# A hybrid decoder layer on one core: turning the next block's rows on VectorE, and branch hints between the job sizes

## What is computed

```
h    = rms_norm(x) * norm_mix
P    = h @ W_in + b_in            -> B_gate | C_gate | u | q | k | v
conv = B_gate * conv3_causal(C_gate * u)
attn = sliding-window attention(QKNorm(q), QKNorm(k), v), 128-query blocks
x    = x + concat(rms_norm(conv), rms_norm(attn)) @ W_out + b_out
x    = x + MoE(rms_norm(x))       top-4 of 32 experts, clamped SwiGLU
```

## Time and profile before

| what | value |
|---|---|
| median of 3 runs | 2038.56 us |
| the profiled execution | 2037.2 us, span 2035.4 us, mean granted TensorE clock 0.990 |
| mixer stage | 0 to about 473 us of the span |
| jobs of over 128 rows | about 501 to 1308 us |
| narrow jobs | about 1308 us to the end |
| TensorE busy | 1977.3 us, 97% of the span |
| VectorE, ScalarE, GpSimd busy | 68%, 19%, 12% |

### The profile page before, as it was taken

How to read it: one execution, slowest core, us unless ns; L and a number is a source line. 1 busy time by engine, 2 the same in 40 slices (tenths; PEclk the granted TensorE clock), 3 DMA queues, 4 the chain that set the end, 5 groups by cost and what they waited for, 6 DMA issues and landing times.

```text
span 2035.4 us, 29772 instructions
## 1 busy us (share of the span) xinstructions
PE 1977.3 (97%) x10588; PEld 1442.1 (71%) x10588; DVE 1385.7 (68%) x3952; ACT 385.3 (19%) x792; POOL 237.5 (12%) x313
## 2 busy tenths in 40 slices
PE   8999999997999999999999999999999999999996
PEld 5777777774999999999999999844444444444443
DVE  2666666663467777778877677687767776677765
ACT  1323233222012122222222222301101010001100
POOL 0221222221010011111111111100000000000000
PEclk9999999998999999999999999999999999999998
DMA  9311110004875687777888888999999999999992
GB/s 302 108 42 41 41 40 12 30 32 182 297 222 198 237 269 243 271 240 274 275 270 286 297 298 289 339 319 366 372 355 363 367 371 362 354 370 369 369 357 76
DMA packets 232241, 504.22 MB, mean 248 GB/s; under 512 B 7428, under 2 KB 14640, under 8 KB 230016
## 3 DMA queue, kind: packets, MB, share of 16 engines
q1 hardware_dynamic: 218496, 454.93, 62.6%
q0 software_dynamic: 11392, 40.18, 8.1%
q10 hardware_dynamic: 2304, 8.39, 1.0%
HBM read 475.48 MB, written 28.00 MB: 247 GB/s over the span
## 4 chain that ended last, share of the span: by engine, by line
issue 44%; PE 26%; DMA 2%; DVE 2%; POOL 1%; ACT 0%; POOLq 0%; DVEq 0%; ACTq 0%
PE ps_unit L1651 26%; DMA out_dram<-y_rows,idx_cur 2%; POOL x_got L1258 1%; DMA x_got<-h_rows,idx_next 0%; DVE act_T L1480 0%; DVE sig L1478 0%; DVE glu L1470 0%; ACT sig L1341 0%; PE ps_list L1623 0%; POOL carrier L1254 0%; POOL out_dram L1302 0%; POOL out_dram L1270 0%; POOLq L1194 0%; DVE match L1391 0%; DVE reached L1435 0%
## 5 line engine op out<-in xcount | busy, mean ns | idle before, releaser
L1651 PE MATMUL ps_unit<-xT,w_slot 128*128 128x136 f32 (+6 forms) x3840 | 526.6, 300 | 10.3 <-issue 8.7
L1651 PEld LDWEIGHTS ps_unit<-xT,w_slot 128*128 128x128 f32 x3840 | 521.3, 197 | 11.5 <-issue 11.4
L1675 PE MATMUL ps_unit<-w_slot,xT 128*128 128x512 f32 x1088 | 473.9, 593 | 0.0
L1675 PEld LDWEIGHTS ps_unit<-w_slot,xT 128*128 128x128 f32 x1088 | 205.3, 190 | 251.6 <-issue 251.6
L1183 DVE STREAM_TRANSPOSE xT<-x_got 32x256 f32<-32x256 f32 x668 | 291.0, 436 | 13.4 <-DMA x_got<-h_rows,idx_next 4.6
L1651 PE MATMUL ps_unit<-act_T,w_slot 128*128 128x136 f32 (+6 forms) x1920 | 264.1, 299 | 7.2 <-DVE act_T L1480 7.1
L1651 PEld LDWEIGHTS ps_unit<-act_T,w_slot 128*128 128x128 f32 x1920 | 259.4, 191 | 10.4 <-DVE act_T L1480 6.3
L1687 PE MATMUL ps_unit<-w_slot,act_T 128*128 128x512 f32 x544 | 239.3, 592 | 1.3 <-DVE act_T L1183 1.3
L1496 DVE STREAM_TRANSPOSE y_rows<-yT 32x256 f32<-32x256 f32 x396 | 172.6, 436 | 42.9 <-ACT yT L1348 37.6
L1183 DVE STREAM_TRANSPOSE act_T<-act_rows 32x64 f32<-32x64 f32 x816 | 192.6, 236 | 12.2
L1687 PEld LDWEIGHTS ps_unit<-w_slot,act_T 128*128 128x128 f32 x544 | 102.0, 190 | 123.6 <-issue 121.5
(11 more groups left out here) (262 smaller groups left out, 1604.3 us busy)
## 6 DMA issues: line engine op xcount, KB each, us to landing
w_slot<-in_w_dram SPq DMA_DIRECT2D x192, 2048.0 KB, 11.0
b_row<-in_b_dram SPq DMA_DIRECT2D x17, 1024.0 KB, 13.0
b_row<-in_b_dram SPq DMA_DIRECT2D x17, 512.0 KB, 15.3
w_in_sb<-in_w_in_dram SPq DMA_DIRECT2D x6, 1024.0 KB, 11.9
x_in<-in_x_dram SPq DMA_DIRECT2D x8, 512.0 KB, 3.4
x_res<-in_x_dram SPq DMA_DIRECT2D x8, 512.0 KB, 4.8
out_dram<-x ACTq DMA_DIRECT2D x8, 512.0 KB, 5.1
h_rows<-h ACTq DMA_DIRECT2D x8, 512.0 KB, 3.1
```

The lines of the kernel that those rows point to most:

```text
L1651: last = pe.matmul(ps_unit[p % RING][:, u, 0:n], w, moving[:, k, 0:n], start=(k == 0), stop=(k == KD - 1))
L1675: last = pe.matmul(ps_hid[c], xT[:, k, 0:P], w_slot[:, c, k, :], start=(k == 0), stop=(k == KD - 1))
```

## The change

Three edits, in both stages.

1. **Rows of the next block.** Squaring (`square_x`) moves to the start of ScalarE's pass and norming (`norm_x`) behind the second u bias; the mean moves behind `add_taps(0)` on VectorE, the reciprocal root to the start of GpSimd's pass. VectorE turns `xn` straight into `hT` in 16 pieces, in three groups of 4, 6 and 6, and ScalarE scales `hT` in place by `norm_mix_col` with 8 instructions. TensorE's two `turn_x` and VectorE's two `read_hT` per pass go, but for block 0. The load of block 1's `x_in` moves up in SyncE's queue, ahead of the store of `rel_rows`, and the two loads in SyncE's loop change places.
[...]
3. **Counts.** Four small matmuls with powers of 64 pack the 12 counts into three numbers; TensorE reads these three words once, between its `hold_clock` matmuls, and unpacks them into registers, in place of one `value_load` before each width.

```
@@ sync
+            wait(sp, x_normed, 0)
+            sp.dma_start(x_in[:], x_rows[P:2 * P, :]).then_inc(x_loaded.sem, 16)
             sp.wait_ge(rel_made, 1)
             sp.dma_start(rel_rows, rel_row).then_inc(rel_stored, 16)
...
-            with sp.Fori(0, NB - 1) as t:
+            with sp.Fori(1, NB - 1) as t:
+                load_residual(t - 1)
                 load_block(t, x_rows[bass.ds((t + 1) * P, P), :])
-                load_residual(t)
+            load_residual(NB - 2)
             load_residual(NB - 1)
@@ gpsimd
+                if more:
+                    rsqrt(x_mean, t + 1, ms_x, rstd_x, x_rstd)
                 add_taps_pool(t, 2)
...
-                if more:
-                    rsqrt(x_mean, t + 1, ms_x, rstd_x, x_rstd)
                 pool.wait_ge(late_loaded, all_late)
@@ scalar
+            def scale_hT(n):
+                wait(act, hT_raw, n - 1)
+                for k in range(KD):
+                    last = nc.scalar.activation(hT[:, k, :], hT[:, k, :], ACT.Copy, scale=norm_mix_col[:, k:k + 1])
+                    if k % 4 == 3:
+                        last.then_inc(hT_ready[k // 4].sem, 1)
...
+                if more:
+                    square_x(t + 1)
                 add_u_bias(t, 0)
...
                 add_u_bias(t, 1)
+                if more:
+                    norm_x(t + 1)
                 exp_half(t, 0)
...
-                if more:
-                    prepare(t + 1)
                 wait(act, attnT_ready, t)
                 nc.scalar.activation(qk_sq[:, 0:AW], ps_c[:, 0, :],
                                      ACT.Square).then_inc(attn_squared.sem, 1)
+                if more:
+                    scale_hT(t + 1)
@@ vector
+            def turn_xn(n, first, count):
+                for s in range(first, first + count):
+                    a, c = s // 4, s % 4
+                    rows = xn[a * 32:(a + 1) * 32, :].rearrange("p (k c j) -> p k c j", c=P // 32, j=32)
+                    last = nc.vector.transpose(hT[c * 32:(c + 1) * 32, :, a * 32:(a + 1) * 32], rows[:, :, c, :])
+                if first + count == 16:
+                    last.then_inc(hT_raw.sem, 1)
...
                 add_taps(t, 0)
+                if more:
+                    x_to_mean(t + 1)
...
                 gate_output(t, 3)
                 if more:
-                    x_to_mean(t + 1)
+                    wait(dve, x_normed, t + 1)
+                    turn_xn(t + 1, 0, 4)
...
                                         ALU.add).then_inc(attn_joined.sem, 1)
+                if more:
+                    turn_xn(t + 1, 4, 6)
...
-                if more:
-                    read_hT(t + 1, 0)
...
+                if more:
+                    turn_xn(t + 1, 10, 6)
                 wait(dve, attn_mixed, t)
...
-                if more:
-                    read_hT(t + 1, 1)
@@ tensor, mixer
                 wait(pe, attnT_ready, t)
-                if more:
-                    wait(pe, x_normed, t + 1)
-                    wait(pe, conv_out[3], t)
-                    turn_x(t + 1, 0)
...
                 if more:
-                    turn_x(t + 1, 1)
                     project_q(t + 1)
@@ experts
+            for i in range(DIGITS):
+                nc.gpsimd.memset(digits[:, i:i + 1], float(1 << BITS * i)).then_inc(digits_made, 1)
...
-            def run_size(v, lo, hi):
-                with pe.If(lo < hi):
+            def run_size(v, lo, hi, skip_hint, next_is_there):
+                jobs_of_size, past_size = f"jobs_of_size_{v}", f"past_size_{v}"
+                skip = pe.br_eq(hi, lo, on_true=past_size, on_false=jobs_of_size)
+                if skip_hint is not None:
+                    skip.branch_hint(skip_hint)
+                hint = None
+                with nc.body(jobs_of_size, valid_engines=[mybir.EngineType.PE]):
...
                     with pe.Fori(lo, hi) as q:
+                        if next_is_there is not None:
+                            hint = pe.mark_branch_hint_location(next_is_there)
                         run_job(q, SIZES[v])
+                    pe.br(past_size)
+                nc.switch_bb(past_size)
+                return hint
...
+            pe.wait_ge(digits_made, DIGITS)
+            for i in range(DIGITS):
+                last = pe.matmul(ps_list[0:1, 3 * P + len(SIZES):3 * P + len(SIZES) + WORDS], digits[:, i:i + 1],
+                                 reached[:, i::DIGITS], start=(i == 0), stop=(i == DIGITS - 1))
+            last.then_inc(keys_spread, 1)
...
-            hold_clock(8)
             pe.wait_ge(table_ready, TABLES)
-            wide = 0
+            words = []
+            for i in range(WORDS):
+                hold_clock(2)
+                words.append(pe.value_load(ends[0:1, len(SIZES) + i:len(SIZES) + i + 1], min_val=0,
+                                           max_val=(1 << BITS * DIGITS) - 1))
+            hold_clock(2)
+            reached_jobs = [pe.snap((words[i // DIGITS] >> BITS * (i % DIGITS)) & ((1 << BITS) - 1)) for i in range(last_size)]
+            wide, hint = 0, None
             for i in range(last_size):
-                reached_jobs = pe.value_load(ends[0:1, i:i + 1], min_val=0, max_val=most_jobs)
-                run_size(last_size - i, wide, reached_jobs)
-                wide = reached_jobs
+                next_is_there = None
+                if i + 1 < last_size:
+                    next_is_there = pe.to_reg(pe.snap(reached_jobs[i] < reached_jobs[i + 1]))
+                hint = run_size(last_size - i, wide, reached_jobs[i], hint, next_is_there)
+                wide = reached_jobs[i]
```

More of the change, by code:

```diff
@@ L276, in mixer @@
         hT_ready = [event("hT_ready_a"), event("hT_ready_b")]
+        hT_raw = event("next_rows_turned")
         qkv_done = event("qkv_done")
@@ L482, in _, with square_x, norm_x @@
         def _(act):
-            def prepare(n):
+            def square_x(n):
                 wait(act, x_loaded, n)
                 nc.scalar.activation(xn[:], x_in[:], ACT.Square, accum_out=ss_x).then_inc(x_squared.sem, 1)
+            def norm_x(n):
                 wait(act, x_rstd, n)
                 nc.scalar.activation(xn[:], x_in[:], ACT.Copy, scale=rstd_x).then_inc(x_normed.sem, 1)
+            def scale_hT(n):
[4 more added lines that the diff above has]
+                        last.then_inc(hT_ready[k // 4].sem, 1)
             def square_qk(n):
@@ L515, in turn_read_act @@
                 nc.scalar.copy(pT[:, i, 1, :], ps_turned[i][1]).then_inc(pT_ready[i][1].sem, 1)
-            prepare(0)
+            square_x(0)
+            norm_x(0)
             act.wait_ge(vectors_ready, 1)
@@ L1011, in experts @@
     most_jobs = NE + S * TOP_K // CAP
+    BITS, DIGITS = 6, 4
+    WORDS = len(SIZES) // DIGITS
+    assert most_jobs < 1 << BITS and len(SIZES) == WORDS * DIGITS
     small = SIZES.index(144)
@@ L1080, in experts @@
         reached = sb("reached", [P, len(SIZES)], BF16)
+        digits = sb("digits", [P, DIGITS], BF16)
         order_key = sb("order_key", [P, 1])
@@ L1084, in experts @@
         order = sb("order", [P, P], BF16)
-        ends = sb("ends", [1, len(SIZES)], I32)
+        ends = sb("ends", [1, len(SIZES) + WORDS], I32)
         ended, started, first, held, size, past = (sb(n, [P, 1]) for n in ("ended", "started", "first", "held", "size", "past"))
@@ L1101, in experts @@
         carrier_cleared = sem("carrier_cleared")
+        digits_made = sem("digits_made")
         buffers = sem("expert_buffers_cleared")
@@ L1447, in _ @@
                                              op0=ALU.is_lt, op1=ALU.mult, accum_out=order_rank[:]))
-            v.tensor_copy(ends[:], ps_list[0:1, 3 * P:3 * P + len(SIZES)]).then_inc(table_ready, 1)
+            v.tensor_copy(ends[:], ps_list[0:1, 3 * P:3 * P + len(SIZES) + WORDS]).then_inc(table_ready, 1)
             v.tensor_tensor(jobs[0:1, 1:2], last_job[0:1, NE - 1:NE],
@@ L1755, in _ @@
             pe.matmul(ps_list[:, 2 * P:3 * P], order_key[:].broadcast_to([P, P]), ident, start=True, stop=True)
-            pe.matmul(ps_list[:, 3 * P:3 * P + len(SIZES)], ones_b[:], reached[:], start=True,
-                      stop=True).then_inc(keys_spread, 1)
+            pe.matmul(ps_list[:, 3 * P:3 * P + len(SIZES)], ones_b[:], reached[:], start=True, stop=True)
+            pe.wait_ge(digits_made, DIGITS)
[3 more added lines that the diff above has]
+            last.then_inc(keys_spread, 1)
             pe.wait_ge(fields_cast, 3)
```

## The result

The changed kernel takes 2027.34 us, the median of 5 runs (2024.96 to 2028.95), against 2042.97 for 5 runs of the kernel before beside it (2037.11 to 2043.55): ratio 0.9934, 95% interval 0.9918 to 0.9949. The profiled execution took 2026.6 us, span 2024.8. Predicted was 2024, range 2018 to 2032.

A forecast was written before the change was run, and what follows sets the result against it. TensorE, busy 97% of the span, was taken as the bound. From 2037.2 us, mixer -2.9 and experts -11.0 (-8.7 - 3.4 + 0.6 + 0.5) gave 2023.3 for the profiled execution; 2024 predicted, 80% range 2018 to 2032.

The forecast's parts named there:

- Jumps and gaps: Experts, TensorE: hinted jumps over empty widths 200, 184 and 160 cost about 0.215 us, so three gaps vanish: -8.7 us.
- Clock behind the gaps: Experts, TensorE: without gaps, two half-rate windows of 3.4 us, each losing 1.7, lose their cause: -3.4 us.
- What takes back in the first job of 152: Experts: VectorE could turn the next rows at 902.4, but their gather lands at 903.0: +0.6 us.
- Ahead of the first job: Experts: extra loads and unpackings delay the first jump, +0.4 us; small matmuls and memsets add +0.1: +0.5 in all.
- The mixer: Mixer: TensorE's transposes go, -6.4 us; waits for turned rows +2.0; later convolution weights at the start +1.5: -2.9 us.
- Turning: Mixer, VectorE and ScalarE: 0.449 us pieces, then scalings; `project_q` waits 0.15 us a pass, 1.0 in block 0: about +2.
- The load moved ahead: Mixer's start, SyncE's queue: `x_in` ahead of the `rel_rows` store makes the awaited convolution weights 1.5 us later: +1.5 us.
- The sum: Whole kernel: 2037.2 - 2.9 - 11.0 = 2023.3 us for the profiled execution; 2024 predicted as median.
- The hint does nothing: Rival, experts: each gap loses only its two loads, 3.9 us in all: 2028, or 2031.5 if the clock falls; 17%.
- The hint costs the loop its own head: Rival, experts: back edges of 8 repeated jobs wait: 2036 at 3.4 us each, 2058 at 6.17; 9%.
- The turned rows come late: Rival, mixer: `project_q` waits 0.8 to 1.5 us a pass and the mixer gives nothing: 2029 to 2033; 6%.

The follow-up runs named there:

- the padding: Changed mixer with the experts of before, plus 17 instructions (waits long fulfilled) at the head of TensorE's code: 2036.93 us, ratio 0.9989 to the kernel before.
- the added copy: Changed kernel without its hints, plus one 2 MB copy within device memory in each wide job, issued by ScalarE: 2051.15 us, one execution.
- one hint less: Changed kernel without the hint for the jump over the empty width 160: 2025.88 us, ratio 0.9933 to the kernel before.

## Why the prediction was right, step by step

*Jumps and gaps (-8.7): right.* The hinted jumps take 0.36, 0.37 and 1.24 us (0.215 was the price taken), the lead of the sequencer covers all three, the gaps are gone. That a hint would do this was the author's estimate, since no row showed a hinted branch. It did: the packets of code are three fewer with three hints (35 for 38), and without the hints the jumps take 3.40 to 3.56 us again.

*Clock behind the gaps (-3.4): right.* In the kernel before TensorE was granted 0.51 of its clock for 3.4 us behind the second gap and behind the third, and 1.00 behind the first:

```profile
574.20:580.00 5.80, 5.80 (x36) 5.80 (x37) 5.62 (x14) 0.00 (x0) 0.00 (x0) 1.00 0.81 303
...
869.90:873.30 3.40, 3.33 (x13) 3.36 (x14) 3.29 (x9) 0.00 (x0) 0.00 (x0) 0.51 1.05 399
```

Both windows at 0.51, this one and that of the earlier trace rows, are gone.

*What takes back in the first job of 152 (+0.6): 2.95, and this is the step that failed, in its path as in its size.* The step let the turned rows come late, behind a gather "released by VectorE after a scatter which does not move". Against the end of TensorE's job before, the scatter's issue did not move (20.3 us behind it, now 20.5), but its landing did: its way to VectorE's copy grew from 6.2 to 9.8 us, since without TensorE's gap the next weights stream beside it (312 GB/s in all in place of 226). VectorE stood 4.12 us in front of the copy with its next clips behind it, and TensorE waited for their result (`act_T`) inside the job, not for turned rows at its end. Holding the weights back brought the scatter to 5.6 us and took 9.75 us off the median, not all of it by way of this scatter.

*Ahead of the first job (+0.5): 0.7, about right in size, for another reason.* The sequencer was in time; the second gather landed some 0.5 us later behind its issue, for a reason that was not tried.

*The mixer (-2.9): -2.0 in this profile, -1.6 to -3.1 in eight others with the same mixer.* Turning came as priced: pieces 0.45, eight scalings 0.3 us each (0.21 would be half of the 256-column one's 0.43, so a fixed part shows), `project_q` waiting 0.17 us a pass (0.15 predicted) and 0.53 in block 0; 0.66 us gained a pass (0.76 predicted). The load moved ahead cost 1.3 (1.5 predicted). Not foreseen was the clock: the stretch at half clock (0.50) at the wait for weights is 6.8 us in place of 3.4 in ten of the eleven profiles with the turn on VectorE and in none of the three with the mixer of before; it was tried only by putting the load back behind the weights, which left it at 6.8, so its cause stays open. TensorE's wait itself is no longer in this profile, 4.50 us for 4.52, because its work ahead of it ran later and slower (`project_q` 10.07 us for 8.83); in the same kernel run again it is 5.39.

*The sum.* On the profiles -10.6 in place of -13.9. The scatter's give-back is 2.4 of the difference and the mixer 0.9; the rest nearly cancels: the gaps gave some 0.6 more than their 8.7, and 0.2 ahead of the first job and 0.4 behind the second of 152 were lost. By medians the change gives more, 0.66% or 13.5 us, because the first profile of before, 2037.2, is one of its faster executions; the sets of runs beside the experiments have medians of 2038.7 to 2041.3. That the gain by medians, 13.5 us, lies so near the 13.9 of the sum owes something to luck: execution against execution only 10.6 of them are there, and what fills them up is the spread of the kernel before, which the sum left out. The one more profile of the kernel before points at the clock: a gap has a tail of clock that varies, and the changed kernel has no gaps to have it behind.

*The rivals.* "The hint does nothing" was priced at 2028, or 2031.5 with the clock. The kernel without hints took 2039.20, outside the whole range: its first two gaps are those priced (1.69 and 1.93 for "1.4 to 1.8"), the third is 8.40, with the second stop that the prediction did not know. Where the code lies otherwise, an unhinted third jump cost a gap of 2.88 us and nothing in the median, so 2039 is the price at this place of the code. "The hint costs the loop its own head" did not happen in any hinted run; its sum was off too, for 3.4 us less a lead of 2 to 2.6 is 0.8 to 1.4 a piece and not 1.3 to 1.9, so 2030 to 2035 instead of 2036. "The turned rows come late" did not either.

**Where the gain would have gone without the hint.** The mixer's half alone shows it: with 17 instructions less, the second piece of code behind a jump is needed before it is there, and a change in another stage costs 5 us. That it is a matter of place is shown by the padding; that this piece is a fetch of its own, which starts late, by its packet in the stop (2.6 and 3.5 us behind the stop's beginning at a share of 0.91 and 0.92, where a jump at a share of at most 0.16 has 1.0). That the traffic is what delays it is shown by an experiment for the jumps alone (the added copy). At which instructions the pieces begin was not measured.

## What to carry to other kernels

A branch over code that isn't executed is worth a hint even when its stall looks small, because its price here (a stop of 3.3 to 6.7 us of the sequencer, and 5 to 6 more for a second piece, less its lead) hung on the traffic at that moment and on where the code lay; two kernels that differ in a remote part are to be compared at their jumps before the difference is believed. When a stall of the main engine goes, list the small transfers that were in flight beside it: bulk loads that have a whole job of slack should wait for an indirect scatter or gather that has none, as holding back one load a job did here (2019.35 us against 2029.10). And a gap cost its length and a stretch at half clock of 3.4 us, 6.8 or none, so one profile of a kernel with gaps may be a lucky one.

## What the runs showed that was not expected

- Length of a gap alone did not decide the fall of the clock: behind 2.88 us ahead of 152 (one hint less) TensorE stayed at 1.00, behind 2.87 ahead of 176 in the kernel before it was granted 0.51, and at the long gaps of 8.21 and 8.40 the stretch at half clock, which begins inside them, is 10.2 us.
- An unhinted jump over an empty width took 3.3 to 3.9 us at a DMA share of at most 0.16 and 5.9 to 6.7 at 1.0, each with a packet of 16 KB on q8 inside it. The second packet behind such a jump stopped the sequencer for another 5.0 and 6.1 us in two kernels; in others, the padded one and the one with one hint less among them, TensorE ran on through it.
- A scatter of 128 and up to 128 rows of 4 KB: 5.6, 6.2, 8.2 and 9.8 us to the copy behind it, at 143, 226, 263 and 312 GB/s. The rate in all does not decide it alone: in the kernel without hints it was 9.2 us at 247.
